# The first block's input projection as three products of rounded halves instead of one plain f32 product

## The chip, the cores and the metric

The kernel runs on one core of a Trainium2 chip. The metric is the time of one execution on the device in microseconds (us), the median of several runs; less is better. The engines: PE (TensorE, matmuls from SBUF into PSUM, which has eight banks of 512 f32 columns), DVE (VectorE), ACT (ScalarE), POOL (GpSimd) and SP (SyncE, which here only issues DMAs). They run their own instruction lists and meet through counting semaphores.

## What is computed

Two transformer blocks, one after the other, on 1024 positions of 1024 features. The change touches the first. Cut to what matters:

```
def first_block(x, ...):
    x = layer_norm(x, ln_emb_g, ln_emb_b)
    z = x @ w_in                      # (1024, 1024) @ (1024, 1984)
    xs, gs, cq, ckv, kr, gm = split(z, (512, 512, 256, 128, 64, 512))
    ys = s5_branch(xs, ...) * silu(gs)            # a state space model
    ym = mla_branch(cq, ckv, kr, ...) * silu(gm)  # attention from latents
    mix = concat([ys, ym]) @ w_out
    u = ALPHA * x + mix
    x = layer_norm(u + sigmoid(u @ w_pg) * (p @ w_pp), ln_g, ln_b)
second_block: ada = silu(c) @ w_ada + b_ada       # (1024,) @ (1024, 6144), ...
```

## The kernel before

Everything is kept transposed: features on the 128 partitions, the 1024 positions along the free axis. A "page" is 1024 f32 per partition, XN is the normalized x in eight pages (k = 0 to 7), and a "tile" is 128 output features by 1024 positions, accumulated over eight k in two PSUM banks. The order of each engine's work is written out by hand.

**Input projection.** `with_ada` (it calls `tile`, line 2768) makes the 16 tiles of z. A tile is 16 plain f32 matmuls of 128x512: for each k, w_in's 128x128 block against both halves of XN[k]. The tiles use banks 0, 1 and 2, 3 in turn. The order is xs (0 to 3), gs (4 to 7), latents q and kv and kr (8 to 11), gm (12 to 15); between them stand the matmuls of the state space model: 32 transposes (line 2841, "x" 0 to 7), 64 small products (2853, x 8 to 15), the chunk inputs (2866, x 16 to 23, which fill SS), and at the end the states, four groups r0 to r3 (2893 and 2901). Each x goes to bank 5 or 6 and is read by ACT before the next but one may start.

**Weights.** SP loads blocks of 512 KB (w_in and w_ada in turn) into a ring of four pages. A block's page is loaded again when `w_used` says that PE has read it.

**Ada.** The second block's modulation is a matrix-vector product that is done on the side: for each of w_ada's column blocks POOL multiplies by silu(c) and adds up in four instructions (`ada_sum`, lines 1439, 1443 twice, 1445), and PE sums over the partitions by a one-column matmul (`ada_column`, line 2781), in the middle of a later tile. PE runs in order, so a tile's second half waits for that column.

**ACT** evicts each tile from PSUM (`z`, line 1663): xs copied in another order of positions, gs and gm through silu to the pages GS and GM, the latents copied. xs goes to DRAM and comes back as UU in another layout (line 1456, POOL's queue). XN goes to DRAM in one DMA of 4 MB right after the layer norm (`xn_dram`, line 1655) and comes back after attention (line 1493).

**DVE** first normalizes x (lines 1108 and 1115), then builds the model's tables: powers of the state matrix, the table W (line 2121, six instructions of 2048 columns), KB (256 columns), the table C (six of 2304 columns, "cp_table"), the table E (16 to 1024 columns) and, after x 15, the skip term of GSB. When SS is filled it does six products, 32 scans, six products ("states ready"); PE's r0 to r3 wait for that. Almost all read two operands from SBUF and each waits for the one before.

After r3 come keys and values (first matmul at line 2768 from page CKV), queries, the gated unit and attention. The output projection `w_out` (line 2803, `products`) already works on split operands: an operand is rounded to fp32r ("high"), the rest is a second operand ("low"), and high x high, high x low and low x high are summed in PSUM.

## Time and profile before

| | us |
|---|---|
| median of 3 runs | 2242.65 |
| lowest and highest | 2240.92, 2244.85 |
| profiled execution | 2246.37 |
| its span, first to last instruction | 2244.4 |

| engine | busy us of the span | share |
|---|---|---|
| PE, matmuls | 2162.1 | 96% |
| PE, weight loads | 1605.4 | 72% |
| POOL | 1187.2 | 53% |
| DVE | 1173.6 | 52% |
| ACT | 753.1 | 34% |

The times in rows of the profile count from the span's first instruction. What stands between span and time (2.0 us) is the start and end of the execution. The input projection with what is woven in takes the stretch from 49 to 304 us. A row of the time line merges instructions of the same kind that follow one another; a plain f32 matmul shows as two records.

### The profile page before, as it was taken

The page shows a single profiled execution, that of the slowest core. Times are in us where ns is not written, and L with a number is a line of the kernel's source. Part 1 is how long each engine was busy: PE and PEld are TensorE (multiplying, and loading weights), DVE is VectorE, ACT ScalarE, POOL GpSimd, SP SyncE. Part 2 cuts the span into 40 slices and gives each one's busy share as a digit, 9 for nine tenths or more (in the row PEclk, how much of TensorE's full clock was granted, in tenths as well). Part 3 has the DMA queues.
Part 4 walks back from the last instruction along what each step waited for, and adds up shares of the span by engine and source line. Part 5 has one row for each costly group of instructions (what it writes and reads, how often), then busy time and mean ns, then how long its engine had stood idle before and what let it go on. Part 6 is the DMA issues. An engine that isn't in the chain of part 4 may idle for free.

```text
span 2244.4 us, 27665 instructions
## 1 busy us (share of the span) xinstructions
PE 2162.1 (96%) x10952; PEld 1605.4 (72%) x10952; DVE 1173.6 (52%) x1492; ACT 753.1 (34%) x1164; POOL 1187.2 (53%) x809
## 2 busy tenths in 40 slices
PE   8999999999998999999999999998999999999998
PEld 3445453787885886568857788876788888878886
DVE  6960664552376413530057425776866666653424
ACT  5111232331014303640055343144554454531211
POOL 2443320308784664435746764373688888844441
PEclk9999999999998999999999999999999999999999
DMA  5434342005321421101211335233122222144112
GB/s 229 175 96 90 73 114 75 10 10 206 113 76 63 143 94 49 41 11 47 87 12 58 113 111 192 91 113 134 45 85 85 85 85 85 57 170 159 47 38 75
DMA packets 63422, 204.51 MB, mean 91 GB/s; under 512 B 14967, under 2 KB 17319, under 8 KB 62479
## 3 DMA queue, kind: packets, MB, share of 16 engines
q1 hardware_dynamic: 52048, 148.54, 20.0%
q10 hardware_dynamic: 8032, 36.45, 4.3%
q0 software_dynamic: 3216, 17.77, 3.2%
q8 instruction: 87, 1.43, 0.3%
q14 instruction: 39, 0.32, 0.0%
HBM read 158.54 MB, written 41.98 MB: 89 GB/s over the span
## 4 chain that ended last, share of the span: by engine, by line
PE 88%; DVE 4%; ACT 4%; issue 2%; POOL 1%; DMA 0%; DVEq 0%; ACTq 0%; SPq 0%
PE ps L3162 21%; PE ps L2803 16%; PE ps L2768 13%; PE ps L3281 11%; PE ps L3086 4%; PE ps L3195 3%; PE ps L3233 2%; PE ps L341 2%; PE ps L511 1%; PE ps L499 1%; PE ps L364 1%; PE ps L1022 1%; PE ps L625 1%; PE ps L636 1%; PE ps L648 1%
## 5 line engine op out<-in xcount | busy, mean ns | idle before, releaser
L1526 POOL TENSOR_TENSOR w_parts<-front,sb_zero 128x1024 fp32r<-128x1024 f32 x69 | 140.7, 2039 | 282.8 <-PE ps L3281 117.7
L3281 PE MATMUL ps<-ffn_parts,w_parts 128*128 128x512 f32 x1008 | 230.3, 389 | 1.5 <-DVE front L2729 1.5
L1601 POOL TENSOR_TENSOR up_parts<-front,up_parts 128x512 fp32r<-128x512 f32 x120 | 194.5, 1627 | 69.6 <-ACT up_parts L1874 69.5
L2768 PE MATMUL ps<-front 128*128 128x512 f32 x512 | 224.3, 595 | 0.0
L1439 POOL TENSOR_TENSOR front<-front,sb_csilu 128x1024 f32<-128x1024 f32 x48 | 103.9, 2164 | 223.3 <-DMA front<-w_ada 223.3
L1531 POOL TENSOR_TENSOR w_parts<-front,w_parts 128x1024 fp32r<-128x1024 f32 x75 | 207.6, 2769 | 23.0 <-ACT w_parts L2029 7.5
L3281 PEld LDWEIGHTS ps<-ffn_parts,w_parts 128*128 128x128 f32 x1008 | 189.0, 188 | 41.8 <-issue 2.6
L3162 PE MATMUL ps<-t_high,up_parts 128*128 128x512 f32 x640 | 204.8, 391 | 4.9 <-ACT back L1881 4.9
L2803 PE MATMUL ps<-h_high,w_parts 128*128 128x512 f32 x672 | 187.7, 394 | 0.6 <-PE ps L3086 0.6
L2768 PEld LDWEIGHTS ps<-front 128*128 128x128 f32 x512 | 95.8, 190 | 114.6 <-issue 114.6
L3162 PE MATMUL ps<-h_high,up_parts 128*128 128x512 f32 x480 | 154.5, 389 | 1.8 <-DVE back L2497 1.8
L3162 PEld LDWEIGHTS ps<-t_high,up_parts 128*128 128x128 f32 x640 | 120.9, 189 | 30.9 <-issue 5.7
L2803 PEld LDWEIGHTS ps<-h_high,w_parts 128*128 128x128 f32 x672 | 124.0, 188 | 25.8 <-issue 1.4
L2679 DVE TENSOR_TENSOR ffn_parts<-back,ffn_parts 128x1024 fp32r<-128x1024 f32 x44 | 70.6, 1612 | 128.8 <-ACT ffn_parts L1999 128.7
L3162 PE MATMUL ps<-t_low,up_parts 128*128 128x512 f32 x320 | 125.2, 391 | 0.0
L1443 POOL TENSOR_TENSOR front<-front 128x512 f32<-128x512 f32 x96 | 116.6, 1214 | 7.5
L2497 DVE TENSOR_TENSOR back<-ps,back 128x512 f32<-128x512 f32 x78 | 53.6, 688 | 113.2 <-PE ps L3162 82.9
L3162 PEld LDWEIGHTS ps<-h_high,up_parts 128*128 128x128 f32 x480 | 90.1, 188 | 20.9 <-issue 2.2
L2803 PE MATMUL ps<-h_low,w_parts 128*128 128x512 f32 x336 | 103.8, 390 | 0.0
L2121 DVE TENSOR_TENSOR back<-back 128x1024 f32<-128x1024 f32 (+10 forms) x61 | 87.8, 1439 | 29.2 <-ACT back L1771 19.8
L1999 ACT ACTIVATE ffn_parts<-back 128x1024 fp32r<-128x1024 f32 x44 | 46.3, 1060 | 158.9 <-PE ps L3281 158.9
L1881 ACT ACTIVATE back<-ps 128x512 f32<-128x512 f32 x98 | 58.6, 598 | 106.0 <-PE ps L3162 100.1
(420 smaller groups left out, 4576.4 us busy)
## 6 DMA issues: line engine op xcount, KB each, us to landing
front<-w_ada SPq DMA_DIRECT2D x48, 512.0 KB, 3.6
front<-w_up SPq DMA_DIRECT2D x44, 512.0 KB, 4.3
front<-w_down SPq DMA_DIRECT2D x22, 512.0 KB, 3.5
front<-w_in SPq DMA_DIRECT2D x16, 512.0 KB, 3.6
front<-w_out SPq DMA_DIRECT2D x16, 512.0 KB, 4.4
residual<-back ACTq DMA_DIRECT2D x2, 4096.0 KB, 15.3
front<-w_gates SPq DMA_DIRECT2D x16, 512.0 KB, 4.1
gates<-back SPq DMA_DIRECT2D x16, 512.0 KB, 3.6
```

What stands on the lines that cost most here:

```text
L1439: pool.tensor_tensor(rows, rows, csilu[:].unsqueeze(2).to_broadcast((P, FT, P)), ALU.mult)\
L1443: pool.tensor_tensor(x[:, 0:w], x[:, 0:w], x[:, w:2 * w], ALU.add).then_inc(S("ada_step"), 1)
L1526: pool.tensor_tensor(high, raw, zero[:, 0:1].to_broadcast((P, PAGE)), ALU.add)\
L1531: pool.tensor_tensor(low, raw, high.bitcast(F32), ALU.subtract).then_inc(S("w_split"), 1)
L1601: pool.tensor_tensor(parts[:, BANK:], src, parts[:, 0:BANK].bitcast(F32), ALU.subtract)\
L2121: link(dve.tensor_tensor(o, a, b, op))
L2679: dve.tensor_tensor(AR[4 + kk % 4], act_at(kk), AR[kk % 4].bitcast(F32), ALU.subtract)\
L2768: mm = pe.matmul(ps[:, bank + nt, :], ring[:, slot, at + k * step:at + k * step + P], rhs(k0 + k)[:, nt * BANK:(nt + 1) * BANK], start=sta ...
L2803: mm = pe.matmul(ps[:, bank + nt, :], w_[:, k * P:(k + 1) * P], x_[k][:, nt * BANK:(nt + 1) * BANK], start=k == 0 and n == 0, stop=k == FT ...
L3086: mm = pe.matmul(ps[:, 2 * j + nt, :], WR[n % 2 + w_][:, at:at + P], x_[2 * b + k][:, nt * BANK:(nt + 1) * BANK], start=b == 0 and k == 0 ...
L3162: mm = pe.matmul(o, parts[:, at + k * P:at + (k + 1) * P], x, start=p in (1, 2, 5) and k == 0 and q == 0, stop=k == 3 and q == 2, skip_gro ...
L3281: mm = pe.matmul(ps[:, 2 * m + nt, :], parts[n % 2 + w_][:, at:at + P], half_of(AR[kk % 4 + x_], nt), start=k == 0 and q == 0, stop=k == N ...
```

## The change

The input projection becomes three products of rounded halves. w_in's block is copied rounded by ACT to pages of its own (`in_high`), and POOL overwrites the block in the ring by the rest (`in_low`). x's rounded half XH is what the layer norm's last step on ACT now writes (to eight other pages), and DVE writes the rest, XL, over XN (`x_low`, with the norm's bias added on the way), once XN is in DRAM. The gain of the norm moves from ACT to DVE's last norm step, where a tensor_tensor becomes a scalar_tensor_tensor; XN in DRAM has no bias yet, and ACT adds it after attention, eight instructions (`x_whole`).

Tile by tile the passes are w_low XH, w_high XH, w_high XL, 16 matmuls each (tile 0 takes the first two together). The first four tiles run only their XH passes at first, in all eight banks, and then their four XL passes; z_tile, which frees and releases everything, comes at the end of a tile's XL pass.

A tile's page in the ring is free after its w_low pass (`win_low_used`), an ada block's after its column (`ada_used`). The blocks are 0 to 3 w_in, then w_ada and w_in in turn (block 4 is ada 0, 5 is tile 4, 6 is ada 1, ..., 27 is tile 15), 28 to 31 w_ada. Tile 4 carries ada columns 0 and 1, tile i from 5 to 15 carries column i - 3 ahead of its w_high pass, and columns 13 to 15 come among the states and the keys.

The order of tiles is xs, gs, gm, then kv, the two of q, and kr last. silu(gs) and silu(gm) no longer stay in pages; each goes to DRAM (`gate`, 512 KB, ACT's queue, two buffers), and POOL's queue brings all back when the projection is through. SS takes the pages of two gate buffers, so ACT waits for gates 4 and 5 to have landed before it copies x 16. The eight DMAs of UU are issued at once after the table C, the skip table GSB now lies in TM's own first rows, so that one of eight TM copies falls away, and DVE's chain after SS works in two halves of eight pairs. Complex products on DVE lose their last copy, and squares take four instructions instead of seven.

```diff
         WR = rounded_pages("w_parts", 34, 4)
+        IN_ORDER = (0, 1, 2, 3, 4, 5, 6, 7, 12, 13, 14, 15, 10, 8, 9, 11)
+        N_IN, IN_FIRST = len(IN_ORDER), 4
+        IN_BLOCK = [i if i < IN_FIRST else 5 + 2 * (i - IN_FIRST) for i in range(N_IN)]
...
+        IN_PAGES = (36, 37, 38, 39, 36, 37, 38, 39, 14, 15, 22, 23, 34, 35, 34, 35)
...
+        def in_high(act, i):
+            act.wait_ge(S(f"w_landed{IN_BLOCK[i] % RING}"), 16 * (IN_BLOCK[i] // RING + 1))
+            if 4 <= i < 8:
+                act.wait_ge(S("z_tile"), i - 3)
+            elif i in (8, 9):
+                act.wait_ge(S("x_in_dram"), 16)
+            elif i in (10, 11):
+                act.wait_ge(S("ssm_ps"), 8)
+            elif i in (12, 13):
+                act.wait_ge(S("ssm_ps"), 24)
+            elif i >= 14:
+                act.wait_ge(S("z_tile"), i - 1)
+            act.activation(IN_HIGH[i], ring[:, IN_BLOCK[i] % RING, :], ACT.Copy).then_inc(S("win_high"), 1)
...
             projected(10, 1, 5)
+            in_high(act, 0)
             projected(11, 1, 6)
+            in_high(act, 1)
...
+                act.activation(XH[k], XN[:, k, :], ACT.Identity, bias=V("ln_emb_b", k)).then_inc(S("norm_ready"), 1)
...
+                x = quarters(XN[:, k, :])
+                dve.scalar_tensor_tensor(x, x, V("ln_emb_g", k), SPREAD, ALU.mult, ALU.mult).then_inc(S("norm_scaled"), 1)
...
+            for i in range(IN_FIRST):
+                load(i, None, *tile_of(t["w_in"], IN_ORDER[i]))
+            for j in range(4):
+                sp.wait_ge(S("norm_scaled"), 2 * j + 2)
+                sp.dma_start(xn_dram[:, 2 * j:2 * j + 2, :], XN[:, 2 * j:2 * j + 2, :]).then_inc(S("xn_in_dram"), 16)
+            def former_used(b):
+                if b - RING in ADA_BLOCKS:
+                    sp.wait_ge(S("ada_used"), ADA_BLOCKS.index(b - RING) + 1)
+                else:
+                    sp.wait_ge(S("win_low_used"), IN_BLOCK.index(b - RING) + 1)
+            for b in range(IN_FIRST, B_UKV):
+                former_used(b)
+                if b in ADA_BLOCKS:
+                    load(b, None, *tile_of(t["w_ada"], ADA_BLOCKS.index(b)))
+                else:
+                    load(b, None, *tile_of(t["w_in"], IN_ORDER[IN_BLOCK.index(b)]))
+            for b, w, m in ((B_UKV, "w_ukv", 0), (B_UQ, "w_uq", 0), (B_UQ + 1, "w_uq", 1), (B_GLU, "w_glu", 0)):
+                former_used(b)
...
+            def in_low(i):
+                pool.wait_ge(S("win_high"), i + 1)
+                pool.tensor_tensor(IN_LOW[i], ring[:, IN_BLOCK[i] % RING, :], IN_HIGH[i].bitcast(F32), ALU.subtract)\
+                    .then_inc(S("win_split"), 1)
...
-                    pool.dma_start(UU[s * GC:(s + 1) * GC, :, :],
-                                   x_dram.rearrange("(g c) t -> c g t", c=GC)[:, :, s * CHUNKS:(s + 1) * CHUNKS])\
-                        .then_inc(S("u_landed"), 16)
-                if a == 12:
-                    pool.wait_ge(S("pool_step"), POOL_STEP["tm_zero"])
+            ada_sum(0)
+            ada_sum(1)
+            in_low(4)
+            in_low(5)
+            for i in range(6, N_IN):
+                ada_sum(i - 4)
+                if i == 9:
+                    pool.wait_ge(S("z_tile"), 8)
+                    pool.memset(TM, 0.0).then_inc(S("pool_step"), 1)
+                in_low(i)
+                if i == 7:
+                    pool.wait_ge(S("x_in_dram"), 16)
+                    pool.wait_ge(S("dve_step"), DVE_STEP["cp_table"])
+                    for s in range(STEP):
...
+            pool.wait_ge(S("gate_out0"), 64)
...
-            act.dma_start(xn_dram, XN).then_inc(S("xn_in_dram"), 16)
+            in_high(act, 2)
+            in_high(act, 3)
...
+            def gate(tile):
+                n = tile - 4
+                at = page((12 if n < 4 else 20) + n % 2)
+                if n >= 2:
+                    act.wait_ge(S(f"gate_out{n % 2}"), 16 * (n // 2))
+                z(tile, at, ACT.Silu)
+                act.wait_ge(S("z_free"), tile + 1)
+                act.dma_start(silu_dram[n], at).then_inc(S(f"gate_out{n % 2}"), 16)
+            z(0, XS[:, 0, :], ACT.Copy)
+            in_high(act, 4)
+            z(1, XS[:, 1, :], ACT.Copy)
+            in_high(act, 5)
+            z(2, XS[:, 2, :], ACT.Copy)
+            z(3, XS[:, 3, :], ACT.Copy)
...
+            in_high(act, 11)
+            gate(9)
+            act.wait_ge(S("gate_out0"), 16 * 3)
+            act.wait_ge(S("gate_out1"), 16 * 3)
...
+            in_high(act, 12)
+            gate(10)
+            in_high(act, 13)
+            gate(11)
+            in_high(act, 14)
+            act.wait_ge(S("gate_out0"), 16 * 4)
+            act.wait_ge(S("gate_out1"), 16 * 4)
+            z(12, CKV, ACT.Copy)
...
+            for k in range(FT):
+                act.activation(XN[:, k, :], XN[:, k, :], ACT.Identity, bias=V("ln_emb_b", k)).then_inc(S("x_whole"), 1)
...
+            dve.wait_ge(S("xn_in_dram"), 64)
+            for k in range(FT):
+                dve.wait_ge(S("norm_ready"), tiles_to("ln_emb", k + 1))
+                dve.scalar_tensor_tensor(XL[k], XN[:, k, :], V("ln_emb_b", k), XH[k].bitcast(F32), ALU.add, ALU.subtract)\
+                    .then_inc(S("x_low"), 1)
...
+            def in_products(bank, parts, x_, start=False, stop=False, ready=None, between=None):
+                for k in range(FT):
+                    if ready:
+                        ready(k)
+                    if between and k in between:
+                        ada_column(between[k], "ada_used")
+                    for n, w_ in enumerate(parts):
+                        for nt in range(2):
+                            mm = pe.matmul(ps[:, bank + nt, :], w_[:, k * P:(k + 1) * P],
+                                           x_[k][:, nt * BANK:(nt + 1) * BANK], start=start and k == 0 and n == 0,
+                                           stop=stop and k == FT - 1 and n == len(parts) - 1)
+                return mm
+            def in_first():
+                for i in range(IN_FIRST):
+                    pe.wait_ge(S("win_split"), i + 1)
+                    if i == 0:
+                        in_products(0, (IN_HIGH[0], IN_LOW[0]), XH, start=True, ready=lambda k:
+                                    pe.wait_ge(S("norm_ready"), tiles_to("ln_emb", k + 1))).then_inc(S("win_low_used"), 1)
+                    else:
+                        in_products(2 * i, (IN_LOW[i],), XH, start=True).then_inc(S("win_low_used"), 1)
+                        in_products(2 * i, (IN_HIGH[i],), XH)
+                for i in range(IN_FIRST):
+                    in_products(2 * i, (IN_HIGH[i],), XL, stop=True,
+                                ready=None if i else lambda k: pe.wait_ge(S("x_low"), k + 1)).then_inc(S("z_tile"), 1)
+            def in_tile(i):
+                bank = 2 * (i % 2)
+                pe.wait_ge(S("win_split"), i + 1)
+                pe.wait_ge(S("z_free"), i - 3 if i < IN_FIRST + 2 else i - 1)
+                in_products(bank, (IN_LOW[i],), XH, start=True).then_inc(S("win_low_used"), 1)
+                if i == IN_FIRST:
+                    pe.wait_ge(S("z_free"), 3)
+                in_products(bank, (IN_HIGH[i],), XH, between={0: 0, 4: 1} if i == IN_FIRST else {0: i - 3})
+                in_products(bank, (IN_HIGH[i],), XL, stop=True).then_inc(S("z_tile"), 1)
...
-            with_ada((12, 14), 0, 0, "z_tile", "z_free", xn)
+            for i in range(10, 14):
+                in_tile(i)
+            latent_sums_pe(pe, 0)
+            in_tile(14)
+            in_tile(15)
+            pe.sem_inc(S("w_used"), B_UKV)
...
-            with_ada((14, 15), 0, 0, "z_tile", "z_free", xn)
-            latent_spread_pe(pe, "q_norm")
-            with_ada((15, 16), 0, 0, "z_tile", "z_free", xn)
```

PE at tiles 4 and 5 of the input projection, before:

```order
L2768 MATMUL ps<-front 128x512 [waits z_free,w_landed0]
L2768 MATMUL ps<-front 128x512 x7
L2781 MATMUL ps<-sb_ones,front 128x1 [waits ada_summed]
L2768 MATMUL ps<-front 128x512 x8
L2768 MATMUL ps<-front 128x512 [waits z_free,w_landed2]
L2768 MATMUL ps<-front 128x512 x7
L2781 MATMUL ps<-sb_ones,front 128x1 [waits ada_summed]
L2768 MATMUL ps<-front 128x512 x8
```

and in the changed kernel at tile 5, from the end of its w_low pass (`w_in_low_98`) over w_high (`w_in_high_86`) to XL (named `h_high` here, whose pages it shares):

```order
L2925 MATMUL ps<-x_high_83,w_in_low_98 128x512 x2
L2925 MATMUL ps<-x_high_84,w_in_low_98 128x512 x2
L2881 MATMUL ps<-sb_ones,front 128x1 [waits ada_summed]
L2925 MATMUL ps<-x_high_77,w_in_high_86 128x512 x2
L2925 MATMUL ps<-x_high_78,w_in_high_86 128x512 x2
L2925 MATMUL ps<-x_high_79,w_in_high_86 128x512 x2
L2925 MATMUL ps<-x_high_80,w_in_high_86 128x512 x2
L2925 MATMUL ps<-x_high_81,w_in_high_86 128x512 x2
L2925 MATMUL ps<-x_high_82,w_in_high_86 128x512 x2
L2925 MATMUL ps<-x_high_83,w_in_high_86 128x512 x2
L2925 MATMUL ps<-x_high_84,w_in_high_86 128x512 x2
L2925 MATMUL ps<-h_high,w_in_high_86 128x512 x16
```

The wait for ada_summed stood in the middle of the 16 matmuls; now it stands after 16 of 48, with 32 behind it.

POOL from ada_sum 2 on, before (each four rows):

```order
L1439 TENSOR_TENSOR front<-front,sb_csilu 128x1024 [waits w_landed1]
L1443 TENSOR_TENSOR front<-front 128x512 [waits ada_step]
L1443 TENSOR_TENSOR front<-front 128x256 [waits ada_step]
L1445 TENSOR_TENSOR front<-front 128x128 [waits ada_step]
L1439 TENSOR_TENSOR front<-front,sb_csilu 128x1024 [waits w_landed3]
L1443 TENSOR_TENSOR front<-front 128x512 [waits ada_step]
L1443 TENSOR_TENSOR front<-front 128x256 [waits ada_step]
L1445 TENSOR_TENSOR front<-front 128x128 [waits ada_step]
```

and in the changed kernel, from the same ada_sum on:

```order
L1472 TENSOR_TENSOR front<-front,sb_csilu 128x1024 [waits w_landed0]
L1476 TENSOR_TENSOR front<-front 128x512 [waits ada_step]
L1476 TENSOR_TENSOR front<-front 128x256 [waits ada_step]
L1478 TENSOR_TENSOR front<-front 128x128 [waits ada_step]
L1483 TENSOR_TENSOR w_in_low_96<-front,w_in_high_87 128x1024 [waits win_high]
L1472 TENSOR_TENSOR front<-front,sb_csilu 128x1024 [waits w_landed2]
L1476 TENSOR_TENSOR front<-front 128x512 [waits ada_step]
L1476 TENSOR_TENSOR front<-front 128x256 [waits ada_step]
L1478 TENSOR_TENSOR front<-front 128x128 [waits ada_step]
L1483 TENSOR_TENSOR w_in_low_98<-front,w_in_high_88 128x1024 [waits win_high]
```

Between two ada_sums there is now an in_low, which waits for ACT's in_high and for which the start of the next tiles waits.

ACT from the last copies of GSB to SS (x 16 to 23), before:

```order
L1686 ACTIVATE back<-ps 16x4x128 [waits ssm_ps] x8
L1663 ACTIVATE back<-ps 128x1024 [waits z_tile] x3
L990 ACTIVATE back<-back 128x1024 [waits z_free,dve_step]
L1663 ACTIVATE back<-ps 128x1024 [waits z_tile]
L1701 ACTIVATE back<-ps 128x512 [waits ssm_ps,u_landed]
L990 ACTIVATE back<-back 128x1024 [waits norm_square_used]
```

and in the changed kernel:

```order
L1759 ACTIVATE back<-ps 16x4x128 [waits ssm_ps] x7
L1087 ACTIVATE w_in_high_92<-front 128x1024 [waits ssm_ps,w_landed3]
L1716 ACTIVATE back<-ps 128x1024 [waits z_tile,gate_out1]
L1732 DMA first_gates<-back 128x1024 [waits z_free]
L1769 ACTIVATE back<-ps 128x512 [waits ssm_ps,gate_out1,gate_out0]
L1769 ACTIVATE back<-ps 128x512 [waits ssm_ps] x7
```

The eviction of x 16 has moved behind gate 5 (line 1716) and its landing in DRAM.

## Rows read from the trace of the kernel before

**Rows 1.** The page: the chain that ended last, and the group of plain tiles.
```profile
PE 88%; DVE 4%; ACT 4%; issue 2%; POOL 1%; DMA 0%; DVEq 0%; ACTq 0%; SPq 0%
...
L2768 PE MATMUL ps<-front 128*128 128x512 f32 x512 | 224.3, 595 | 0.0
```

**Rows 2.** Stretches: busy us (instructions) per engine, clock, DMA share, GB/s.
```profile
49.00:304.00 255.00, 252.78 (x881) 122.87 (x880) 154.20 (x251) 46.75 (x54) 91.66 (x73) 1.00 0.40 110
538.00:583.00 45.00, 45.00 (x204) 37.35 (x203) 4.88 (x4) 4.25 (x4) 35.03 (x26) 1.00 0.28 94
```

**Rows 3.** Time line of PE: start, duration, line, [idle before].
```profile
49.14 20.76 PE L2768 MATMUL ps<-front 128*128 128x512 f32 x48
69.74 0.28 PE L2781 MATMUL ps<-sb_ones,front 128*128 128x1 f32 x2
...
83.70 0.28 PE L2781 MATMUL ps<-sb_ones,front 128*128 128x1 f32 x2
...
318.75 1.98 PE L2768 MATMUL ps<-back,front 128*128 128x512 f32 x4
```

**Rows 4.** Time line of PE: two ada columns of the output projection, one tile apart.
```profile
538.75 0.28 PE L2781 MATMUL ps<-sb_ones,front 128*128 128x1 f32 x2
...
549.88 0.28 PE L2781 MATMUL ps<-sb_ones,front 128*128 128x1 f32 x2
```

**Rows 5.** Time line of ACT: a tile's eviction, and one of x 16.
```profile
219.75 1.02 ACT L1663 ACTIVATE back<-ps 128x1024 f32<-128x1024 f32 x1 [12.93 <-PE ps L2768]
...
235.38 0.60 ACT L1701 ACTIVATE back<-ps 128x512 f32<-128x512 f32 x1 [0.64 <-PE ps L2866]
```

**Rows 6.** Time line of POOL: two ada_sums, and low halves of another stage.
```profile
87.58 3.74 POOL L1439 TENSOR_TENSOR front<-front,sb_csilu 128x1024 f32<-128x1024 f32 x1 [7.32 <-DMA front<-w_ada]
...
97.93 2.65 POOL L1445 TENSOR_TENSOR front<-front 128x128 f32<-128x128 f32 x1
...
129.38 1.90 POOL L1439 TENSOR_TENSOR front<-front,sb_csilu 128x1024 f32<-128x1024 f32 x1 [8.11 <-DMA front<-w_ada]
...
133.53 0.49 POOL L1445 TENSOR_TENSOR front<-front 128x128 f32<-128x128 f32 x1
...
407.82 2.35 POOL L1490 TENSOR_TENSOR mix_low<-back,mix_high 128x1024 fp32r<-128x1024 f32 x1
```

**Rows 7.** Time line of DVE: the tables W and C, small instructions, the states' chain.
```profile
61.70 13.93 DVE L2121 TENSOR_TENSOR back<-back 128x2048 f32<-128x2048 f32 x6
...
89.60 7.67 DVE L2121 TENSOR_TENSOR back<-sb_ptab,back 128x2304 f32<-128x2304 f32 x2
...
101.95 4.41 DVE L2121 TENSOR_TENSOR sb_small<-sb_small 128x16 f32<-128x16 f32 x7
...
106.60 1.42 DVE L2121 TENSOR_TENSOR sb_small<-sb_small 128x16 f32<-128x16 f32 x7
...
247.57 16.38 DVE L2121 TENSOR_TENSOR back<-back 128x2048 f32<-128x2048 f32 x6
...
294.88 0.07 DVE L2293 MEMSET back<- 128x16 f32 x1
```

**Rows 8.** DMA: a load beside ACT's 2 MB write, its reader; XN's write (us to landing).
```profile
111.92 0.33 SPq L1267 DMA_DIRECT2D front<-w_ada  x1
116.70 1.90 POOL L1439 TENSOR_TENSOR front<-front,sb_csilu 128x1024 f32<-128x1024 f32 x1 [10.38 <-DMA front<-w_ada]
...
embedded<-front ACTq DMA_DIRECT2D x1, 4096.0 KB, 15.8
```

**Rows 9.** Time line of DVE: first uses of x after attention.
```profile
518.53 1.22 DVE L2370 SCALAR_TENSOR_TENSOR front<-front,ps 128x1024 f32<-128x1024 f32 x1 [2.31 <-PE ps L2803]
533.51 1.22 DVE L2370 SCALAR_TENSOR_TENSOR front<-front,ps 128x1024 f32<-128x1024 f32 x1 [13.76 <-PE ps L2803]
```

**Rows 10.** Stretches as in rows 2, right behind gaps of PE of 2 us.
```profile
355.00:359.00 4.00, 3.62 (x6) 1.67 (x7) 0.24 (x1) 3.99 (x5) 0.00 (x0) 0.70 0.19 77
520.00:524.00 4.00, 3.53 (x9) 2.82 (x10) 0.00 (x0) 0.84 (x1) 3.84 (x4) 0.57 1.04 446
```

311 lines of the change are left out of this document (155 added, 156 removed).

## Prediction

> **What bounds the kernel now.** I read the chain of work that ended last first: 88% of the span is on TensorE (PE) [rows 1]. The costliest group before attention is line 2768, the input projection in plain f32: 224.3 us for its 16 tiles [rows 1]. The table of stretches shows PE busy 252.78 of the 255 us from 49 to 304 us, at full clock [rows 2], while the vector engine (DVE) is busy 154 us, POOL 92 and ACT 47. So in this stage every microsecond taken from PE comes off the end, until something that feeds PE is late. Between PE and the next stages there is no slack either: the matmuls that follow the projection end where the first key/value matmul starts, at 318.75 us [rows 3], and the attention needs all of them.
>
> **Part 1, the products.** A plain tile with its ada column takes 83.70 - 69.74 = 13.96 us [rows 3]: 16 matmuls of 0.864 us and 0.14 us of column. The new tile is 48 matmuls on rounded operands, as the first block's output projection runs them already: from one ada column to the next 549.88 - 538.75 = 11.13 us for 48 products, 0.227 us each without the column [rows 4], PE busy 45 of 45 us there [rows 2]. The order (w_low x_high, w_high x_high, w_high x_low as whole passes) changes neither the count nor the weight load that every matmul has. Gain 16 x (13.96 - 11.13) = 45.3 us. The Trainium skill (FP8 and Floating Point Precision, section TensorE Precision Notes) counts true FP32 as four passes through the array; three of the four would be 13.82 x 3/4 = 10.4 us a tile, and 8 us more gain in all than the rows' 10.88 without a column; the trace is nearer to three passes and a twentieth more.
>
> **Part 2, what feeds the products.** Each tile now needs one ACT copy (in_high, 1.02 us for that shape [rows 5]) and one POOL subtraction (in_low, 2.35 us [rows 6]) on top of POOL's ada_sum. Undisturbed, POOL's ada_sum takes 133.53 + 0.49 - 129.38 = 4.6 us, so POOL needs 7 us per tile of 11.1: it fits. But POOL and DVE get in each other's way when both read two operands of SBUF. Where DVE ran 2304-wide instructions, one ada_sum took from 87.58 to 100.58, 13.0 us, as each of its four steps waited for a DVE instruction of 2.56 us. And DVE lost about 3.0 of ada_sum's 4.6 us: 7 small instructions took 4.41 us beside it and 1.42 us without [rows 7], and the two of 5.1 us took 7.67. So I count 3.0 us of DVE per ada_sum and 2.0 per in_low (its 2.35 less 0.35, what each of ada_sum's four steps left over).
>
> DVE's queue gets later, in this order: its table work would go on at 61.7 [rows 7]. Ahead of it now stand in_low 2 and 3 (4.0) and most of ada_sum 0 (2.8), to 68.5. The new wait for x in DRAM is over by then: four writes of 1 MB are issued from 44 to 51 us, the single 4 MB write took 15.8 [rows 8], and even with pp's 2 MB beside it that is 44 + 1.5 x 15.8 = 67.7. Then x_low, 8 x 1.23 us (a scalar_tensor_tensor of that shape took 1.22 [rows 9]) and ada_sum 1: to 81.2. PE starts at 49.1 as now [rows 3], runs four tiles of 32 products (29.0 us) to 78.1 and takes x_low k by k until 81.5. I put its wait at 0, but there is no slack: each microsecond there counts. The tables follow: 13.9 for W [rows 7] and in_low 4 and 5 (4.0), to 99.1; the wide C table runs from about 105 to 126.
>
> **Where PE waits: the ada column of tile 5.** PE finishes the four tiles at 92.7 and tile 4 at 103.8. Block 8 (ada 2) can be loaded only when tile 4's ada column has read block 4, at 96.5 (92.7 + 3.6 + 0.2). A load beside a 2 MB write of ACT took 116.70 - 111.92 = 4.8 us to its reader [rows 8], and x's write to DRAM is under way again: 101.8 allowing for block 9. ada_sum 2 then falls on DVE's 256-wide instructions and the C table: between 4.6 (free) and 13.0 us (all wide); laid beside DVE's queue it is 11.2, to 113.0. PE wants its column at 103.8 + 3.6 + 0.3 = 107.7: it waits 5.3 us. Behind this matmul stand two thirds of tile 5, and through it the load of block 12. in_low 6 (2.35 and a 2.2 wait) and ada_sum 3 (10) end at 127.6 where tile 6 wants them at 125.9: 1.7 us. Tile 7: 1.0 us. Sum 8.0 us, between 0 and 15. After tile 7 DVE's instructions are narrow or waiting, and POOL gains 3 to 4 us per tile; I find in_low 8 to 15 early by 5 us or more, though tile 14 and 15 wait for in_high behind the tile before.
>
> **Where PE waits: the states' input (x 18).** ACT may write SS only when gates 4 and 5 have landed in DRAM. After tile 9 it evicts (1.02), issues, and waits 3.6 us and the semaphores, then copies bank 5 (0.60 [rows 5]): 5.4 us. PE has two groups of about 1.0 us to do; it waits 3.4 us. Lower bound 0 (if gate 5 were early), upper 5 beside a block's load.
>
> **The clock.** After a gap of 2 us and more the granted clock is 0.57 and 0.70 for the next 4 us [rows 10]: part of that stretch at 1.2 GHz instead of 2.4. That costs 1.2 to 1.7 us a gap; two gaps, 3.4 us.
>
> **Parts at nothing.** The DVE chain of the states takes 294.95 - 247.57 = 47.4 us [rows 7]; now it begins at 198 and with POOL's locks (12 us) ends at 258, while PE comes for it at 265. Its cover is 7 us. The gate write and read go on free queues. XN's bias, 8 x 1.2 us on ACT after x comes back, ends at about 528: x is back by 518.53, the first use now; PE's third tile needs that use when its second tile is done, at 533.51 [rows 9]. Cover 4 us. Behind r3 the gains of q's latents stand ahead of k_high on ACT: PE waits 1.2 us more there.
>
> **Sum.** 45.3 - 8.0 - 3.4 - 3.4 - 1.2 = 29.3 us. The profiled execution, 2246.37 us (span 2244.4), would be 2217.1; against the median of the runs, 2242.65, it is 2213.4 us.
>
> **Rivals.** (a) Forecast, 0.56: 2213.4. (b) The columns are in time, chance 0.20: ada_sum 2 falls before the C table (x_low early, or blocks landing sooner). For it: the phase decides, and one ada_sum at 129.38 took 4.6 us. Against: the wide work is 21 us long and lies where block 8 lands. 45.3 - 3.4 - 1.7 - 1.2 = 39.0, 2203.7. (c) The lock costs more and x_low is late, 0.17: x_low ends 3 to 5 us later, PE waits that long and its clock falls once more, and every table comes later by it: 21 to 24 us gained, 2219 to 2222; with tiles 8 and 9 hit as well (5 us) 2226. The page SBUF — State Buffer of the Trainium skill, section Who interferes with whom, says that the loser blocks for the whole instruction. The rows agree for POOL (13.0 us), but DVE loses 3.0 of 4.6 us. By the whole instruction DVE's queue loses 1.6 us more per ada_sum and 0.35 per in_low, PE waits some 8 us longer, and the time is 2221. (d) POOL becomes the bound, chance 0.04, the side of slower: where all its steps wait for wide DVE instructions it needs 13.0 + 4.9 = 17.9 us per tile against PE's 11.1. If that held for the 11 tiles from 5 on, 11 x 6.8 = 75 us would be lost and the kernel would be 30 us slower, 2272; it decides from 7 such tiles on. Against: DVE has wide work for about 65 us of this stage, five or six tiles at most, and PE takes some of it with slack. (e) The change doesn't do what it says, 0.03: the products run at 0.29 us, as a plain tile's time over 48, because the weight loads are not hidden in the new order; then nothing is gained, the smaller waits stay, and it is 2247. Against: [rows 2, 4].
>
> **Chances and range.** About 0.2% (4.5 us) is what a measurement can tell from no change. Faster 0.93 (a, b, c), same 0.02 (half of e), slower 0.05 (d, the rest of e). The range holds (a) with its bounds (columns 0 to 15 us), (b) and (c): 2201 to 2226.
>
> **What would show it.** The tiles' pitch of 11.1 us on PE with 0.227 us a product; gaps on PE at the ada column of tiles 5, 6 and 7 released by POOL, one ada_sum of 9 to 13 us from about 102; a gap of 3 to 4 us two groups into the eight that fill SS, released by ACT; a granted clock under 0.8 behind them; the last state matmul at 286 to 291 us instead of 318.8; nothing moved afterwards but that offset. A wait of PE for x_low, or waits for win_split in tiles 10 to 15, would speak for (c) and (d); a PE with no gap before tile 8 for (b).

## The result

| | before | after |
|---|---|---|
| median, us (4 runs each, side by side) | 2243.75 | 2231.57 |
| lowest and highest | 2240.92, 2246.72 | 2228.83, 2233.53 |
| profiled span | 2244.4 | 2231.7 |

The ratio is 0.9944, with a 95% interval from 0.9932 to 0.9956: the change is faster, by 12.2 us. The forecast was 29.3 us faster and a time of 2213.4 us; 2231.6 lies above its range of 2201 to 2226. The direction was right, the size was not.

### The profile page after: what moved, and what is told of

It is laid out like the page before. It is cut to its first block, busy times and chain, and to the rows that moved or that the text cites. A ratio compares the mean times of both kernels' runs of the same rounds, so it can differ in the third digit from the quotient of the medians.

```text
span 2231.7 us, 28169 instructions
## 1 busy us (share of the span) xinstructions
PE 2122.7 (95%) x11208; PEld 1656.5 (74%) x11208; DVE 1226.7 (55%) x1476; ACT 777.9 (35%) x1188; POOL 1235.6 (55%) x826
## 4 chain that ended last, share of the span: by engine, by line
PE 83%; DVE 7%; ACT 3%; POOL 2%; issue 2%; DMA 2%; SPq 0%; ACTq 0%; DVEq 0%
PE ps L3292 22%; PE ps L2903 16%; PE ps L3411 11%; PE ps L2925 6%; PE ps L3216 4%; PE ps L3325 3%; PE ps L2868 3%; PE ps L3363 2%; PE ps L355 2%; PE ps L525 1%; PE ps L513 1%; PE ps L378 1%; PE ps L1036 1%; PE ps L507 1%; PE ps L538 1%
## 5 line engine op out<-in xcount | busy, mean ns | idle before, releaser
L1579 POOL TENSOR_TENSOR w_parts<-front,sb_zero 128x1024 fp32r<-128x1024 f32 x69 | 140.4, 2034 | 282.6 <-PE ps L3411 117.7
L2203 DVE TENSOR_TENSOR back<-back 128x1024 f32<-128x1024 f32 (+10 forms) x72 | 102.9, 1429 | 51.6 <-ACT back L1769 22.3
L1483 POOL TENSOR_TENSOR w_in_low<-front,w_in_high 128x1024 fp32r<-128x1024 f32 x16 | 43.9, 2751 | 112.8 <-ACT w_in_high L1087 112.8
L3292 PE MATMUL ps<-h_low,up_parts 128*128 128x512 f32 x240 | 93.4, 389 | 0.0
```

The source lines that it names most:

```text
L1579: pool.tensor_tensor(high, raw, zero[:, 0:1].to_broadcast((P, PAGE)), ALU.add)\
L2203: link(dve.tensor_tensor(o, a, b, op))
L3292: mm = pe.matmul(o, parts[:, at + k * P:at + (k + 1) * P], x, start=p in (1, 2, 5) and k == 0 and q == 0, stop=k == 3 and q == 2, skip_gro ...
```

## The profile after

The page's engines and the chain that ended last:

```profile
PE 2122.7 (95%) x11208; PEld 1656.5 (74%) x11208; DVE 1226.7 (55%) x1476; ACT 777.9 (35%) x1188; POOL 1235.6 (55%) x826
PE 83%; DVE 7%; ACT 3%; POOL 2%; issue 2%; DMA 2%; SPq 0%; ACTq 0%; DVEq 0%
```

The stretch from the first tile to the last state matmul, which answers to [rows 2] (busy us and instructions of PE, weight loads, DVE, ACT and POOL, then PE's clock, DMA share, GB/s):

```profile
49.00:308.00 259.00, 231.56 (x1318) 190.33 (x1316) 214.71 (x243) 67.18 (x77) 147.06 (x97) 0.93 0.44 129
```

PE's share of the chain fell from 88% [rows 1] to 83%. Before, PE had 2 us of idle time from 49 to 304 us; now it has 27 in 259, at a mean clock of 0.93. The time line of PE (start, duration, line, [idle before, and what ended it]) says where. First the fifth to the eighth tile and the transposes:

```profile
82.44 11.62 PE L2925 MATMUL ps<-h_high,w_in_high 128*128 128x512 f32 x50 [0.47 <-DVE h_high L2289]
...
116.92 0.58 PE L2881 MATMUL ps<-sb_ones,front 128*128 128x1 f32 x2 [7.86 <-POOL front L1478]
117.36 6.13 PE L2925 MATMUL ps<-x_high,w_in_high 128*128 128x512 f32 x16
...
130.61 0.28 PE L2881 MATMUL ps<-sb_ones,front 128*128 128x1 f32 x2
130.75 3.90 PE L2925 MATMUL ps<-x_high,w_in_high 128*128 128x512 f32 x16
...
149.44 1.03 PE L2969 MATMUL ps<-sb_ident,back 128*128 128x128 f32 x8
162.52 5.12 PE L2969 MATMUL ps<-sb_ident,back 128*128 128x128 f32 x24 [12.05 <-ACT back L1751]
```

then the filling of SS, two ada columns one tile apart, and the states:

```profile
206.51 7.17 PE L2994 MATMUL ps<-back 128*64 128x128 f32 x96 [3.26 <-ACT back L1769]
...
217.39 0.28 PE L2881 MATMUL ps<-sb_ones,front 128*128 128x1 f32 x2
...
228.52 0.28 PE L2881 MATMUL ps<-sb_ones,front 128*128 128x1 f32 x2
...
299.78 2.51 PE L998 MATMUL ps<-back,sb_pick 32*128 32x256 f32 x8 [3.63 <-DVE back L1018]
302.22 3.78 PE L3020 MATMUL ps<-back 128*128 128x128 f32 x16
...
308.14 1.98 PE L2868 MATMUL ps<-back,front 128*128 128x512 f32 x4
```

The tiles do what was forecast: 228.52 - 217.39 = 11.13 us from column to column, and x_low held PE for 0.47 us only. But five gaps, 0.47 + 7.86 + 12.05 + 3.26 + 3.63 = 27.3 us, stand between. Behind four of them the granted clock is low (0.56 from 116 to 123 us, 0.63 from 162 to 168, 0.79 from 206 to 214, 0.62 from 299 to 308), and the same matmuls take longer: 6.13 instead of 3.90 us, 5.12 instead of 3.45 (three times the 1.15 us that eight such transposes take at full clock), 7.17 instead of 5.55 (as in the run with copies first, below), and 2.51 + 3.78 instead of 1.47 + 2.05 us: 2.2 + 1.7 + 1.6 + 2.8 = 8.3 us. 45.3 - 27.3 - 8.3 = 9.7 us; the keys start at 308.14 instead of 318.75 us [rows 3], 10.6 us earlier.

Of these 10.6 us, 9.4 are left when the values start (320.15 instead of 329.56), as PE waits 1.1 us longer for k_low. That the span gained 12.7 us is no work of the change: in attention the distance grows by 1.6 us, and by 1.6 again at the start of the output projection, where both kernels do the same on PE. Both times it is the clock, which happened to be low before and not after; in attention (stretches, columns as above):

```profile
409.00:411.00 2.00, 2.00 (x7) 1.61 (x6) 0.35 (x1) 0.00 (x0) 2.00 (x2) 0.50 0.00 0
```

and in the kernel after, at the same instructions:

```profile
398.00:400.00 2.00, 1.73 (x11) 1.59 (x12) 1.34 (x6) 1.10 (x4) 1.92 (x2) 1.00 0.00 0
```

The gap of 12.05 us was in no term of the forecast. Its chain stands on ACT and on the queues of POOL and SP (time lines):

```profile
139.42 0.33 ACTq L1732 DMA_DIRECT2D first_gates<-back  x1
159.50 1.06 ACT L1087 ACTIVATE w_in_high<-front 128x1024 fp32r<-128x1024 f32 x1 [20.11 <-DMA front<-w_in]
160.46 1.01 ACT L1716 ACTIVATE back<-ps 128x1024 f32<-128x1024 f32 x1
161.50 0.33 ACTq L1732 DMA_DIRECT2D first_gates<-back  x1
161.87 1.09 ACT L1751 ACTIVATE back<-ps 128x512 f32<-128x512 f32 x2 [0.40 <-ACT back L1716]
...
131.75 5.26 POOL L1503 DMA_DIRECT2D back<-ssm_in_by_feature  x8
...
141.92 0.33 SPq L1299 DMA_DIRECT2D front<-w_in  x1
```

PE's third group of transposes waits for ACT's first copy of PW, the pages that take the transposes out of PSUM (line 1751). ACT stands at in_high 9 (line 1087) until 159.5, for block 15, whose load SP issued at 141.92: 17.6 us, where the 16 loads of w_in have a median of 3.7. Between these times the eight DMAs of UU were under way, all issued at 131.75; the median from issue to landing was 7.3 us before and is 14.5 now, and the DMA engines are full (called the flood below; stretch, the last but one number is their share):

```profile
142.00:159.00 17.00, 8.47 (x42) 6.89 (x41) 15.66 (x40) 0.00 (x0) 10.08 (x6) 0.82 1.02 164
```

## The experiments

Two things are to be told apart for the large gap: the DMAs that make the load late, and the order on ACT that lets gate 7 and the copies of PW stand behind an instruction that waits for it. Each ratio is to the kernel before, run beside the version. That kernel's median was 2243.75, 2243.17, 2243.73 and 2243.64 us in the four sets of runs, so versions of different sets are compared by their medians.

**Copies first.** ACT's order alone:

```diff
             for tile in range(4, 8):
                 gate(tile)
-                if tile < 7:
+                if tile < 6:
                     in_high(act, tile + 3)
...
+            in_high(act, 9)
             in_high(act, 10)
             gate(8)
```

> ACT takes in_high 9 behind gate 7 and the eight copies of PW instead of ahead of them; the eight DMAs of UU stay bunched. Theory 1 (both are needed for the gap: the late load and what is queued on ACT behind the instruction that waits for it): block 15 still lands some 17 us after its issue, but only in_high 9 and low half 9 wait for it, which PE wants about 178 us at the latest; no gap at the transposes, 2217.5 us. Theory 2 (the flood delays PE by itself as well, for instance through tile 8's weights, an ada column or UU): a gap of 5 to 12 us appears elsewhere before 180 us, 2222 to 2232 us.

Measured: 2220.48 us, ratio to before 0.9903 (0.9886 to 0.9919), 11.1 us less than the changed kernel. Block 15 still comes only at 159.5 us, but PE doesn't wait for it:

```profile
141.12 0.33 SPq L1299 DMA_DIRECT2D front<-w_in  x1
...
159.53 1.06 ACT L1087 ACTIVATE w_in_high<-front 128x1024 fp32r<-128x1024 f32 x1 [3.82 <-DMA front<-w_in]
...
151.24 1.15 PE L2970 MATMUL ps<-sb_ident,back 128*128 128x128 f32 x8 [1.30 <-ACT back L1751]
```

Theory 1 holds; 1.7 us of small waits for the copies stayed, which the expectation did not have.

**UU in three parts.** POOL's order alone:

```diff
-                if i == 7:
+                if i == 8:
                     pool.wait_ge(S("x_in_dram"), 16)
                     pool.wait_ge(S("dve_step"), DVE_STEP["cp_table"])
-                    for s in range(STEP):
+                if 8 <= i < 11:
+                    for s in range(3 * (i - 8), min(3 * (i - 7), STEP)):
```

> The eight DMAs of UU leave POOL's queue three, three and two at a time, behind the low halves 8, 9 and 10, instead of all at once behind low half 7; nothing else is changed. Theory 1 (the eight at once fill the DMA engines, and the load of block 15, tile 9's weights, issued at 141.9 us, lands at 159 instead of some 146; ACT stands at in_high 9 for it, with gate 7 and the copies of PW behind it, and PE at the third transpose group): the load of block 15 takes 4 to 6 us, the gap of 12.05 us at the transposes is under 1 us, and the 24 transposes take 3.1 us instead of 5.1 as the clock does not fall; 2231.6 - 12.0 - 2.0 = 2217.5 us. Theory 2 (the gap comes from the order on ACT or from a late gate, whatever the DMAs do): the gap stays over 8 us, the time 2228 to 2233 us.

Measured: 2225.0 us (2220.3 to 2230.6), ratio 0.9912 (0.9894 to 0.9931). Half a hit: the load issued at 141.44 beside the first three DMAs (138.51) was there at 151.79, 10.3 us later, and a gap of 5.03 us remained.

```profile
138.51 2.15 POOL L1504 DMA_DIRECT2D back<-ssm_in_by_feature  x3
...
151.79 1.06 ACT L1087 ACTIVATE w_in_high<-front 128x1024 fp32r<-128x1024 f32 x1 [12.88 <-DMA front<-w_in]
...
154.81 5.11 PE L2970 MATMUL ps<-sb_ident,back 128*128 128x128 f32 x24 [5.03 <-ACT back L1752]
```

**UU at once, but later**, behind low half 9 (`if i == 9`), ACT's order as in the changed kernel:

> The changed kernel with the eight DMAs of UU still all at once, but behind low half 9 instead of low half 7, some 16 us later on POOL's queue (about 148 instead of 132 us); ACT's order is unchanged. Theory 1 (the flood delays whichever block of weights is being loaded, and PE waits where ACT stands for that block): block 15 is in place in time and the gap of 12 us at the transposes is gone or under 2 us, but block 17, for in_high 10, issued at some 158 us, lands only with the flood's end at 168 to 175 us, and since the copies of x 8 stand behind in_high 10 on ACT, a gap of 3 to 10 us opens two groups into x 8 to 15: 2221 to 2227 us. Theory 2 (only the place behind low half 7 was bad): no new gap, 2218 us.

Measured: 2241.73 us (2233.2 to 2246.0), ratio 0.9988 (0.9977 to 1.0), 10.2 us more than the changed kernel. The mechanism came as theory 1 has it, and it cost far more than its 2221 to 2227 us. Block 15 (issued 140.18) was there at 143.72, in 3.5 us. Block 17 (issued 157.36) took 19.6 us, and the gap moved to the group that stands behind in_high 10 (time lines of POOL, SP, ACT and PE):

```profile
153.54 5.25 POOL L1503 DMA_DIRECT2D back<-ssm_in_by_feature  x8
...
157.36 0.33 SPq L1299 DMA_DIRECT2D front<-w_in  x1
...
176.92 1.06 ACT L1087 ACTIVATE w_in_high<-front 128x1024 fp32r<-128x1024 f32 x1 [22.62 <-DMA front<-w_in]
...
179.99 16.29 PE L2982 MATMUL ps<-back 64*16 64x128 f32 x96 [11.98 <-ACT back L1759]
```

```profile
180.00:196.00 16.00, 16.00 (x96) 11.21 (x96) 0.00 (x0) 3.35 (x6) 4.68 (x5) 0.50 0.07 27
```

The surprise is PE's row and the stretch under it: behind the gap PE ran all 96 small products at half clock (0.50, the lower of its two levels, 1.2 of 2.4 GHz), 16.29 us instead of 8.4 (three quarters of the 11.20 us for 128). The clock stayed at 0.50 with PE busy throughout until about 202 us, and the tile behind lost another 2.5 us (13.87 us up to SS instead of 11.39).

**The kernel before with UU at once**, to see whether the flood needs anything of the change:

```diff
-                for s in range(2 * (a - 8), min(2 * (a - 7), STEP)):
+                for s in range(STEP if a == 8 else 0):
```

> The kernel before with one edit: the eight DMAs of UU are issued at once ahead of ada_sum 8 instead of two ahead of each of ada_sum 8 to 11. Theory 1 (it is the eight at once that fill the DMA engines, with nothing of the changed kernel needed for it): they land 10 to 23 us after their issue instead of 5 to 9, and the loads of blocks issued beside them take 10 to 17 us instead of 3.6; here POOL and PE wait for such a block too, so 5 to 12 us are lost: 2249 to 2256 us. Theory 2 (the loads were late in the changed kernel because gates and x go to DRAM at the same time): loads stay under 7 us, 2242 to 2246 us.

Measured: 2244.3 us, ratio 1.0006 (0.9997 to 1.0015): no difference; the time is theory 2's, and theory 1's price was wrong. The DMAs did land late, 12.7 us in the median instead of 7.3, with no gates in sight. But no load fell among them: SP issued one at 153.43, 0.4 us ahead of the eight, which landed in 5.1 us, and the next at 178.52, since PE is at transposes and small products in between. So the long landings come from the eight at once; what they cost hangs on who loads then. That the flood delays a load is shown by the kernels above, not by this one. Theory 2's other half, that a gate's write delays a load by itself, does not fit the changed kernel's own trace: a load issued at 130.80 us, 2.6 us behind the write of a gate (128.24), landed in 3.6 us.

**Early columns.** Ada columns 0 and 1 at the start of tile 4's first pass:

```diff
-                in_products(bank, (IN_LOW[i],), XH, start=True).then_inc(S("win_low_used"), 1)
                 if i == IN_FIRST:
                     pe.wait_ge(S("z_free"), 3)
-                in_products(bank, (IN_HIGH[i],), XH, between={0: 0, 4: 1} if i == IN_FIRST else {0: i - 3})
+                in_products(bank, (IN_LOW[i],), XH, start=True, between={0: 0, 1: 1} if i == IN_FIRST else None)\
+                    .then_inc(S("win_low_used"), 1)
+                in_products(bank, (IN_HIGH[i],), XH, between=None if i == IN_FIRST else {0: i - 3})
```

> Ada columns 0 and 1 stand at the start of tile 4's w_low pass instead of in its w_high pass, so that blocks 8 and 10 can be loaded 3.6 and 5.7 us earlier. Theory 1 (the stall of 7.9 us at tile 5 comes from block 8, landed at 105 us; but what PE gains there it gives back at the transposes, whose gap ends when block 15 lands out of the flood of UU's DMAs, whenever PE comes): ada_sum 2 starts at 98 to 101 instead of 105.15 us, the stall at tile 5 falls to 0 to 3 us, the gap at the transposes grows from 12 to 15 to 19 us, and the time moves by less than 4 us: 2228 to 2232 us. Theory 2 (the two stalls are independent): the gap at the transposes stays at 12 us and the time falls by 7.9 - 1.5 and 2 us of clock, to 2223 us.

Measured: 2229.07 us (2228.3 to 2229.8), ratio 0.9937 (0.992 to 0.9954). ada_sum 2 starts at 98.34 instead of 105.15 us, and tile 5 no longer waits, but the stall turned up at tiles 6 and 7, and the gap at the transposes ended when it did in the changed kernel (161.75 and 162.52 us):

```profile
125.14 0.59 PE L2881 MATMUL ps<-sb_ones,front 128*128 128x1 f32 x2 [4.43 <-POOL front L1478]
...
141.65 0.38 PE L2881 MATMUL ps<-sb_ones,front 128*128 128x1 f32 x2 [3.05 <-POOL front L1478]
...
161.75 5.50 PE L2970 MATMUL ps<-sb_ident,back 128*128 128x128 f32 x24 [9.84 <-ACT back L1751]
```

The time fits theory 1, its way only in part: the gap at the transposes didn't grow, since POOL's next sums had already taken back what tile 5 gained.

**Both edits**, three parts and early columns:

> Both edits together: UU's DMAs three, three and two at a time, and ada columns 0 and 1 at the start of tile 4. Theory 1 (what the early columns gain is kept once no gap behind them takes it back): stalls at tiles 5 to 7 together 0 to 4 us instead of 7.9, no gap at the transposes, 2217.5 - 6 to 9 = 2208 to 2212 us. Theory 2 (POOL's own work, not block 8, sets the pace from tile 5 to 7: ada_sum 2 merely meets more of DVE's wide instructions when it starts earlier): stalls of 6 us and more stay at tiles 5 to 7, 2215 to 2218 us.

Measured: 2218.36 us, ratio 0.9889 (0.9873 to 0.9906): the time is that of theory 2 (2215 to 2218), the stalls at tiles 5 to 7, 4.45 us, lie between the two. The gap at the transposes is gone but for 1.7 us; tile 6's column waits 4.45 us. POOL shows why: ada_sum 3 took from 111.26 to 124.76, 13.5 us, beside DVE's table C, where an undisturbed one takes 4.6.

```profile
111.26 4.22 POOL L1472 TENSOR_TENSOR front<-front,sb_csilu 128x1024 f32<-128x1024 f32 x1
115.55 6.48 POOL L1476 TENSOR_TENSOR front<-front 128x512 f32<-128x512 f32 x2
122.11 2.65 POOL L1478 TENSOR_TENSOR front<-front 128x128 f32<-128x128 f32 x1
```

**Table C in quarters**, with copies first, three parts and early columns. The seven instructions of 2304 columns become 28 of 576:

```diff
-            tt(Q0, A0, C0, ALU.mult)
...
+            for part in range(4):
+                q0, q1, a0, a1, c0, c1, t_ = (x[:, 4 * part:4 * part + 4] for x in (Q0, Q1, A0, A1, C0, C1, tc))
+                tt(q0, a0, c0, ALU.mult)
...
```

> Copies of PW ahead of in_high 9, UU's DMAs three, three and two at a time, ada columns 0 and 1 at the start of tile 4, and DVE's table C in four parts of four pairs each: 28 instructions of 576 columns instead of 7 of 2304. Theory 1 (POOL's sums are late at tiles 5 and 6 because each of its steps waits for a DVE instruction of 2304 columns, so that shorter ones cost it less): ada_sum 3 takes 6 to 9 us beside the table instead of 13, the stall of 4.5 us at tile 6's column falls under 1.5 us, DVE's table takes 22 to 26 us as before and its end at 130 us at most holds nobody; 2218.4 - 1.7 (the small waits at the transposes) - 3.5 to 5.5 = 2211 to 2213 us. Theory 2 (POOL loses the same share of the time whatever the size of DVE's instructions): ada_sum 3 stays at 11 us and more, the stall at 3 us and more, 2215 to 2217 us.

Measured: 2213.71 us (2212.4 to 2214.7), ratio 0.9871 (0.9855 to 0.9887). PE has no gap over 0.5 us from 49 us to the transposes at 140. Theory 1 is right that size matters; its second half, that the table's later end holds nobody, is not: PE already waits 1.87 us at 261.36 for ACT's square of q's latents (line 1004), which stands behind "states ready", and the run of all six edits shows more of it.

**No wait for gates 4 and 5**, on top of copies first:

```diff
             gate(9)
-            act.wait_ge(S("gate_out0"), 16 * 3)
-            act.wait_ge(S("gate_out1"), 16 * 3)
```

> On top of the copies of PW ahead of in_high 9: ACT no longer waits for gates 4 and 5 (of tiles 8 and 9, in pages 20 and 21) to have landed before it copies x 16 to SS (pages 12 to 15, in which gates 0 to 3 stood, for whose landing ACT has waited already ahead of gates 2 to 5). Theory 1 (this wait alone holds PE two groups into x 16 to 23): the gap of 3.3 us there is gone or under 0.3 us, and the time falls by 3.3 and up to 1.5 us of clock: 2216 to 2217 us against 2220.5. Theory 2 (what is gained there is lost again where the chain of the states and the latents ends, since DVE's chain, not PE, sets the start of the states): DVE gets SS earlier by the same 3.3 us, so this would show as a wait for states that is longer by what DVE lost; 2220 us.

Measured: 2214.33 us (2213.3 to 2214.9), ratio 0.9871 (0.9854 to 0.9887), 6.1 us less than with copies first alone. The gap went from 3.38 to 0.28 us, and the trace's later rows up to 686 us are 3.6 us earlier; the other 2.5 us of the median are about what medians here differ by (with copies first alone the four runs lie at 2217.5 to 2223.2). Theory 1. The wait guarded nothing: SS lies in pages 12 to 15, and gates 4 and 5 in 20 and 21.

**The reciprocal within the angle**, on top of copies first:

```diff
-            reduce_angle(COS, SIN)
-            dve.sem_inc(S("dve_step"), 1)
+            link(dve.tensor_scalar(SIN, COS, 1.0 / _TWO_PI, ROUND, ALU.mult, ALU.add))
+            link(dve.tensor_scalar(SIN, SIN, ROUND, None, ALU.subtract))
             latent_rstd_dve(dve, "q_norm")
+            for part in (TP1, TP2, TP3):
+                link(dve.scalar_tensor_tensor(COS, SIN, -part, COS, ALU.mult, ALU.add))
+            link(dve.tensor_scalar(COS, COS, PI_IN, -PI_IN, ALU.min, ALU.max))
+            dve.sem_inc(S("dve_step"), 1)
             latent_dve(dve, "q_norm", (1, 2))
...
-                if x == 27:
+                if x == 29:
                     act.wait_ge(S("dve_step"), DVE_STEP["angle_reduced"])
```

> On top of the copies of PW ahead of in_high 9: DVE takes the reciprocal of q's root after four of the eight instructions of the rotary angle instead of behind all of them, and ACT takes the two sines behind x 29 instead of x 27. Theory 1 (the gap of 3.6 us at q's spread, released by DVE's reciprocal, comes from the order on DVE alone): the gap is gone, the 16 matmuls behind it take 2.05 us instead of 3.8, and the time falls by 5 us, to 2215.5 us against 2220.5. Theory 2 (the angle is then late, and ACT's sines or the copies of x 28 and 29 hold PE at the last states or the first keys instead): gaps of 2 us and more there, 2218 to 2220 us.

Measured: 2221.6 us (2215.7 to 2223.2), ratio 0.9899 (0.9881 to 0.9917): nothing gained. The gap of 3.6 us is gone and the values start at 301.86 instead of 305.79 us. But then DVE stands 7.75 us at the DMA of kr, and PE waits 4.33 us ahead of the second query tile, where with copies first alone it does not wait at all (both kernels wait 2.46 us ahead of the third); the 16 matmuls behind take 8.72 instead of 7.1 us:

```profile
285.62 0.92 POOL L1520 DMA_DIRECT2D back<-first_gates  x1
286.53 0.74 POOL L1521 DMA_DIRECT2D back<-first_gates  x1
293.59 0.54 POOL L1525 DMA_DIRECT2D back<-back  x1 [6.33 <-DVEq L2415]
...
309.46 3.75 DVE L2204 TENSOR_TENSOR back<-back 128x1024 f32<-128x1024 f32 x3 [7.75 <-DMA back<-back]
...
321.14 8.72 PE L2873 MATMUL ps<-back,front 128*128 128x512 f32 x16 [4.33 <-DVE q_low L2431]
```

**And the gates read last**, on top of that. The two reads of the gates (4 MB) moved on POOL's queue behind the copies of kr and the way of y through DRAM:

> On top of q's reciprocal within the angle's instructions, which won 3.9 us up to the values and lost it again at the queries: the reads of the gates from DRAM (4 MB, POOL's queue) are issued behind those of kr and y instead of ahead of them. Theory 1 (DVE stood 7.8 us at kr's copies, which queue behind these 4 MB, and q_low was late by it): kr's copies land 4 to 8 us after their issue, DVE does not wait for them past the keys, the gap at the second query tile is 2.5 us instead of 4.3, and the time is 2215 to 2217 us against 2221.6. Theory 2 (the gates come too late for the gated unit now): a gap of PE ahead of or in the attention, 2218 us and more.

Measured: 2211.4 us (2210.5 to 2212.5), ratio 0.9858 (0.9843 to 0.9873), 10.2 us less. kr was there at 299.46, 7.3 us behind its last copy's issue (292.19) instead of 14.3, and the gap of 4.33 us is 0.49:

```profile
299.46 3.74 DVE L2204 TENSOR_TENSOR back<-back 128x1024 f32<-128x1024 f32 x3 [0.76 <-DMA back<-back]
...
314.28 7.10 PE L2873 MATMUL ps<-back,front 128*128 128x512 f32 x16 [0.49 <-DVE q_low L2431]
```

Theory 1 is right on the cause and too low on the gain; the 2.5 us that it leaves at the second tile belong to the third. Of the 10.2 us the traces show 7.1 in the rows at 689 us: 3.8 between the values and attention, and 3.0 ahead of the values, 1.4 of them by a full clock behind SS (5.55 instead of 6.99 us). The remaining 3 us of the median are not explained.

**All six edits** (copies first, three parts, early columns, quarters, no gate wait, the reciprocal):

> All six edits together: copies of PW ahead of in_high 9, UU's DMAs in three parts, the early columns, table C in quarters, no wait for gates 4 and 5, q's reciprocal within the angle's instructions. Theory 1 (the four waits are what the forecast lacked, and each is independent of the rest once the one behind it is gone): no gap over 1.5 us on PE from 49 us to the last state matmul, and 2212 - 3.3 - 5 = 2203 to 2205 us. Theory 2 (DVE's chain of the states, which had 3.5 us to spare, is late now): a wait of some us for states ready, 2206 to 2210 us.

Measured: 2212.01 us (2210.4 to 2214.2), ratio 0.986 (0.9843 to 0.9876). Theory 2, and worse than its number. With the waits gone and the table in quarters, DVE is the bound:

```profile
261.76 1.08 PE L983 MATMUL ps<-back,sb_ones_q 128*32 128x256 f32 x8 [5.43 <-ACT back L1004]
262.77 2.51 PE L998 MATMUL ps<-back,sb_pick 32*128 32x256 f32 x8
265.21 3.78 PE L3027 MATMUL ps<-back 128*128 128x128 f32 x16
```

ACT's square of q's latents (line 1004) stands behind "states ready". In quarters, POOL's ada_sum 3 took 6.3 us beside table C instead of 13.5, but the table itself went from 106.99 to 140.4, 33.4 us instead of 23.6; table E behind it ended at 195.4 instead of 182, and the states' chain began when SS was long full. The quarters are the likely reason: the best version takes the waits away without them and has no such gap.

**Best.** All but the quarters; the gates read last; gate 7 behind the copies of PW; and against the stall at tile 6, POOL takes low half 7 ahead of ada_sum 3 and PE takes that column in the last pass of the tile:

```diff
-                ada_sum(i - 4)
+                if i != 7:
+                    ada_sum(i - 4)
...
                 in_low(i)
+                if i == 7:
+                    ada_sum(3)
...
+                in_products(bank, (IN_HIGH[i],), XL, stop=True, between={6: 3} if i == 6 else None).then_inc(S("z_tile"), 1)
```

> All that helped, without table C in quarters (which made DVE's tables 13 us later and its chain of the states PE's bound): the copies of PW ahead of gate 7 and in_high 9, UU's DMAs in three parts, early ada columns 0 and 1, no wait for gates 4 and 5, q's reciprocal within the angle, the gates read behind kr and y; new is that POOL takes low half 7 ahead of ada_sum 3, and PE takes tile 6's column in its last pass, 6 us later. Theory 1: no gap over 1.5 us on PE between 49 us and the last state matmul; against six edits' 2212.0 us the wait of 5.4 us for the states and its 3 to 4 us of clock are gone: 2202 to 2205 us. Theory 2 (the stall at tile 6 only moves to low half 7 or to tile 7's column): a gap of 2 to 5 us there, 2206 to 2209 us.

Measured: 2204.97 us (5 runs, 2203.7 to 2206.4), ratio 0.9828 (0.9815 to 0.9841), 38.7 us under the kernel before and 26.6 under the changed one. The time is theory 1's. One gap of theory 2 is there, 4.16 us at tile 6's column (ada_sum 3 still had 12.3 us beside table C), but from 49 to 282 us PE is busy 227 of 233, at full clock nearly throughout (stretch):

```profile
49.00:282.00 233.00, 227.24 (x1326) 185.80 (x1325) 221.56 (x242) 69.71 (x81) 146.69 (x95) 0.99 0.44 128
```

## Why the prediction missed, point by point

- **The products** were right: 11.13 us per tile, 0.227 us each, 45.3 us gained. (The forecast's 10.88 us for a tile without its column leaves out 0.11 us that the pass behind the column takes longer, 3.74 instead of 3.63; its sum goes by 11.13 and is not touched.) Rival (e) is out.
- **x_low** was right, 0.47 us of wait against 0 forecast with no slack. Rival (c), a late x_low, did not come.
- **Tile 5's column** was right in place and cause, and low by 2.6: 7.86 us instead of 5.3. Block 8 landed 7.3 us after its issue at 97.83 instead of the 5.3 (96.5 to 101.8) that the forecast gave it. Tiles 6 and 7 did not wait (2.7 us forecast), as the longer stall in front of them gave POOL the time. The sum of the three, 7.9, meets the forecast's 8.0 by luck: one term was 2.6 too low, the others 2.7 too high. That tiles 6 and 7 only had slack by tile 5's stall, the early columns showed.
- **SS** was right: 3.26 us against 3.4.
- **"Parts at nothing" failed**, and with it the forecast. It said that "the gate write and read go on free queues" and did not speak of UU's DMAs at all, though the change's own text had them at once instead of two at a time. They cost 12.05 us, plus 1.7 of clock, since block 15 took 17.6 us and gate 7 and the copies of PW stood on ACT behind the instruction that waits for it. The step left out was to ask what else is loaded in the 23 us that they run, and who stands behind it on ACT. The same sentence was wrong on the gates' read: it is what kr's copies wait behind, unseen as long as DVE comes later than they do.
- **DVE's cover failed too.** The states' chain took 278.5 - 214.4 = 64 us instead of 60, which PE still did not feel (it came at 282); but what stands behind the chain on DVE, the angle's instructions and then q's reciprocal, ended 3.63 us late. The forecast stopped its count at "states ready".
- **The clock**: two gaps at 1.7 us were forecast, 3.4; four gaps took 8.3. Both the price per gap was low (1.2 to 1.7 us; it was 1.6 to 2.8) and the number of gaps, half of what came.
- **kv's queue**: 1.2 us forecast; PE waits 1.73 us for k_low instead of 0.63, 1.1 more.

Against the forecast that leaves 12.05 (transposes) + 3.63 (q's spread) + 4.9 (clock) - 0.1 (the columns) + 0.5 (x_low) - 0.1 (SS) = 20.9 us more lost up to the keys. The forecast had the keys' start at 318.75 - 30.5 = 288.3 us, and it is 308.1: 19.8 us. The remaining 1 us is not assigned. The clock's luck in attention and the output projection gave some 3 us back in the profiled span. None of the rivals named this cause; the time lies between (c), at most 2226, and (e), 2247.

Rival (d), POOL as the bound, was right in its mechanism and wrong in its reach: POOL needs 12 to 13.5 us for a sum beside wide instructions, but only for as long as table C runs. That, and not block 8 alone, is why 4 us at tile 6 are left in the best version.

## What to carry to other kernels

A change of order on a DMA queue is priced by everyone who loads while it runs: list the transfers in flight for the whole time that the moved ones take, and for each that could be late, what is queued behind the instruction that waits for it. A cover must be counted down to the last instruction of the queue that hides there, and each wait that is taken away shows the next: here the flood hid POOL's pace, the late reciprocal hid the gates' read, and the gaps hid DVE's chain. An instruction that waits for a transfer belongs behind those that don't.
